# Routing of a mixture-of-experts layer: experts compared in every group beside the group choice, running counts by doubling, slot positions of the chosen experts only, one-hot tables in halves, single-pass products

## What is computed

```python
p_group = softmax(t @ w_rg + b_rg); top_p, top_g = top_k(p_group, 1)
inner_logits = einsum('td,gde->tge', t, w_re) + b_re
sel_logits = einsum('tge,tg->te', inner_logits, one_hot(top_g))
top_l, top_e = top_k(sel_logits, 2); top_w = softmax(top_l)
gate = one_hot(top_g) * top_p  x  sum_k top_w[k] * one_hot(top_e[k])
for e in range(16):
    a, u = split(t @ w_ei[e], 2)
    y += gate[:, e] * ((silu(a) * u) @ w_eo[e])
```

## Time and profile before

| | us |
|---|---|
| median of 3 runs | 1457.71 (1456.18 to 1462.59) |
| profiled execution, its own time | 1458.04 |
| its span in the profile | 1456.3 |

### The profile page before, as it was taken

How to read it: one execution, slowest core, us unless ns; L and a number is a source line. 1 busy time by engine, 2 the same in 40 slices (tenths; PEclk the granted TensorE clock), 3 DMA queues, 4 the chain that set the end, 5 groups by cost and what they waited for, 6 DMA issues and landing times.

```text
span 1456.3 us, 20186 instructions
## 1 busy us (share of the span) xinstructions
PE 1291.3 (89%) x7662; PEld 1074.6 (74%) x7663; DVE 787.1 (54%) x956; ACT 640.7 (44%) x872; POOL 271.7 (19%) x279
## 2 busy tenths in 40 slices
PE   5999998899998999998899997388999999899960
PEld 4788756788798888756688797366787778778850
DVE  3333488321664432378421665577856775985546
ACT  2322456422322322465422322367745564775434
POOL 0432000000200232000000200134522323652210
PEclk9999999999999999999999997589999999999985
DMA  7773300044572444300045563379977987996416
GB/s 173 230 168 87 87 1 2 1 93 138 127 221 88 93 107 90 87 1 2 1 88 144 119 206 122 135 244 309 329 222 224 335 263 258 314 362 221 139 36 244
DMA packets 58464, 222.41 MB, mean 153 GB/s; under 512 B 12087, under 2 KB 12599, under 8 KB 50935
## 3 DMA queue, kind: packets, MB, share of 16 engines
q1 hardware_dynamic: 43088, 177.40, 40.9%
q0 software_dynamic: 12192, 34.51, 8.4%
q10 hardware_dynamic: 3116, 9.54, 1.7%
HBM read 200.19 MB, written 34.32 MB: 161 GB/s over the span
## 4 chain that ended last, share of the span: by engine, by line
PE 71%; DVE 11%; ACT 7%; issue 6%; DMA 3%; POOL 1%; SPq 0%; ACTq 0%; POOLq 0%; DVEq 0%
PE banks L658 20%; PE banks L659 20%; PE banks L660 20%; ACT qkvA L1159 2%; PE banks L868 2%; ACT moe_hi L1199 2%; PE banks L940 2%; DVE pt L1451 2%; DVE moe_lo L1341 1%; PE banks L792 1%; PE banks L826 1%; PE banks L861 1%; DVE neg_max L1419 1%; DMA raw<-in_front_w 1%; POOL gated L567 1%
## 5 line engine op out<-in xcount | busy, mean ns | idle before, releaser
L1341 DVE TENSOR_TENSOR moe_lo<-moe_raw,moe_hi 128x2048 fp32r<-128x2048 f32 x102 | 233.1, 2289 | 78.9 <-ACT moe_hi L1199 75.8
L1354 DVE TENSOR_TENSOR wlo<-raw,whi 128x2048 fp32r<-128x2048 f32 (+1 forms) x52 | 116.1, 2232 | 185.2 <-ACT whi L1049 185.2
L1199 ACT ACTIVATE moe_hi<-moe_raw 128x2048 fp32r<-128x2048 f32 x102 | 194.7, 1914 | 43.6 <-PE banks L660 38.9
L658 PE MATMUL banks<-xT,whi 128*128 128x512 f32 x448 | 175.2, 391 | 0.0
L659 PE MATMUL banks<-xT,whi 128*128 128x512 f32 x448 | 175.0, 391 | 0.0
L660 PE MATMUL banks<-xT,wlo 128*128 128x512 f32 x448 | 175.0, 391 | 0.0
L658 PE MATMUL banks<-moe_lo,xeh 128*128 128x512 f32 x368 | 148.1, 403 | 9.0 <-issue 4.7
L658 PE MATMUL banks<-wlo,xT 128*128 128x256 f32 x512 | 148.8, 291 | 6.9 <-DVE xT L1478 6.7
L659 PE MATMUL banks<-whi,xT 128*128 128x256 f32 x512 | 146.6, 286 | 0.0
L660 PE MATMUL banks<-whi,xT 128*128 128x256 f32 x512 | 146.5, 286 | 0.0
L659 PE MATMUL banks<-moe_hi,xeh 128*128 128x512 f32 x368 | 145.5, 396 | 0.0
(11 more groups left out here) (242 smaller groups left out, 2422.0 us busy)
## 6 DMA issues: line engine op xcount, KB each, us to landing
moe_raw<-in_expert_w SPq DMA_DIRECT2D x192, 512.0 KB
raw<-in_front_w SPq DMA_DIRECT2D x104, 512.0 KB, 6.8
toeplitz_rows<-bias_rows POOLq DMA_DIRECT2D x4, 1152.0 KB, 15.8
kqv<-in_x SPq DMA_DIRECT2D x8, 512.0 KB, 10.9
pt<-in_x SPq DMA_DIRECT2D x2, 2048.0 KB, 9.5
x_rows<-pt ACTq DMA_DIRECT2D x8, 512.0 KB, 2.7
token_sums<-pt ACTq DMA_DIRECT2D x8, 512.0 KB, 3.6
sum_tile<-token_sums SPq DMA_DIRECT2D x8, 512.0 KB, 8.6
```

Of the source, the lines that this page charges most:

```text
L658: mm(dst, left[0], right[1], start=first, stop=False)
L1199: A(moe_hi[m % SPLIT_E], moe_raw[m % RAW_E], ACT.Copy).then_inc(e_hi, 1)
L1341: V.tensor_tensor(moe_lo[m % SPLIT_E], moe_raw[m % RAW_E], moe_hi[m % SPLIT_E].bitcast(F32), ALU.subtract).then_inc(e_lo, 1)
L1354: V.tensor_tensor(view(lo, shape), view(raw[c % 2], shape), view(hi, shape).bitcast(F32), ALU.subtract).then_inc(w_split, 1)
```

## The change

It rewrites the routing and moves work around it.

- The best and the second expert are sought in all four groups at once (128x128 tiles), beside the search for the group; `run` and `done` let two such chains take turns on DVE.
- Running counts come from three additions of 128x128 (`pairs`, `fours`, `upto_t`) in place of eight of 128x16. The rank product waits for the membership, the one for the counts for a second signal; DVE's next step waits for these two products and no longer for the totals.
- Positions are worked out for the 16 chosen pairs of tile and choice only, from rank and base by two multiply-and-sum steps.
- `hot_lo` and `hot_col` are made in halves of 128x1024, in turns; ACT and PE start on a half. `hot_token` and `hot_col` are stored as fp32r, so that the token products are one pass of TensorE each.
- Gates and the experts' counts are worked out behind the one-hots, counts behind the slot table.
- DVE splits two weight chunks ahead of the routing and two behind the slot table; ACT puts the last `store_x1` and `keep_x1` between its first three splits.
- POOL issues the second pair of gathers when the first pair has landed.

```diff
-            nc.alloc_sbuf_tensor_at(name, [P, 2 * NT * P], F32, offset=place_at)[:, :].rearrange("p (n i) -> p n i", n=2 * NT)
-            for name, place_at in (("hot_lo", hot_at), ("hot_gate", hot_at + W_BYTES),
-                                   ("hot_col", late_at), ("hot_token", late_at + W_BYTES))]
+            nc.alloc_sbuf_tensor_at(name, [P, 2 * NT * P], dt, offset=place_at)[:, :].rearrange("p (n i) -> p n i", n=2 * NT)
+            for name, dt, place_at in (("hot_lo", F32, hot_at), ("hot_gate", F32, hot_at + W_BYTES),
+                                       ("hot_col", F32R, late_at), ("hot_token", F32R, late_at + W_BYTES))]
...
             pool.wait_ge(x1_out, 16 * NT + 1)
             for b in range(2):
+                if b == 1:
+                    pool.wait_ge(rows_in[0], 32)
                 for c in range(2):
                     nc.gpsimd.indirect_dma_start(
                         out=x_rows[b][:, c * D:(c + 1) * D], out_offset=None, in_=x1_d[:, :],
...
-            mm(bank[2][:, 0:M16], before, rt[:, 0:M16], start=True, stop=False)
-            mm(bank[2][:, 0:M16], ones, rt[:, M16:2 * M16], start=False, stop=True)
-            mm(bank[3][:, 0:NE], ones, rt[:, 2 * M16:2 * M16 + NE], start=True, stop=True).then_inc(ranked, 1)
+            mm(bank[2][:, 0:M16], before, member_t, start=True, stop=False)
+            pe.wait_ge(member, 2)
+            mm(bank[2][:, 0:M16], ones, upto_t, start=False, stop=True).then_inc(ranked, 1)
+            mm(bank[3][:, 0:NE], ones, upto_t[:, M16 - NE:M16], start=True, stop=True).then_inc(ranked, 1)
             for a in range(2):
                 for n in range(2 * NT):
-                    pe.wait_ge(hot_ready, 2)
+                    pe.wait_ge(hot_ready, 2 + 2 * (n // NT))
                     pe.wait_ge(weighted, 2 * NT * a + n + 1)
-                    last = mm(bank[4 + a][:, 0:FULL_COL], hot_w[a][:, n], hot_col[:, n], start=(n == 0), stop=(n == 2 * NT - 1))
+                    last = mm(bank[4 + a][:, 0:FULL_COL], hot_w[a][:, n], hot_col[:, n] if a == 0 else hot_col[:, n].bitcast(F32),
+                              start=(n == 0), stop=(n == 2 * NT - 1))
                 last.then_inc(tabled, 1)
...
-                if s == SEQS - 1:
-                    store_x1(s, 3)
-                    keep_x1(s, 3)
...
-            for c in range(EARLY_E):
-                e_split(0, c)
+            e_split(0, 0)
+            store_x1(SEQS - 1, 3)
+            e_split(0, 1)
+            keep_x1(SEQS - 1, 3)
+            e_split(0, 2)
...
             for k, weight in enumerate((token, gate)):
-                act.wait_ge(hot_ready, 1)
                 for n in range(2 * NT):
+                    act.wait_ge(hot_ready, 1 + 2 * (n // NT))
...
-                    for c in range(EARLY_E):
-                        e_split(0, c)
+                    for o in (0, R_PAIRS - 4 * NE, R_FOURS - 4 * NE):
+                        V.memset(rt[:, o:o + 4 * NE], 0.0).then_inc(zeroed, 1)
+                    V.memset(small[:, 58:60], 0.0)
+                    e_split(0, 0)
+                    e_split(0, 1)
...
-            chain(V.memset(rt[:, M16:M16 + NE], 0.0))
-            for j in range(1, NT + 1):
-                o = M16 + j * NE
-                ins = V.tensor_tensor(rt[:, o:o + NE], rt[:, o - NE:o], rt[:, (j - 1) * NE:j * NE], ALU.add)
-                if j < NT:
-                    chain(ins)
-            ins.then_inc(member, 1)
...
+            n_e = run(V.tensor_reduce(t4(best), lg_e, X, ALU.max))
+            n_g = run(V.tensor_reduce(g_max, lg_g, X, ALU.max))
+            done(n_e)
+            n_e = run(V.tensor_tensor(t44(e_tmp), lg_e, over_e(best), ALU.is_equal))
+            done(n_g)
+            n_g = run(V.tensor_tensor(t4(g_tmp), lg_g, over_4(g_max), ALU.is_equal))
+            V.tensor_tensor(t4(g4), lg_g, over_4(g_max), ALU.subtract).then_inc(r_exp_in, 1)
+            done(n_e)
+            n_e = run(V.tensor_tensor(t44(e_tmp), t44(e_tmp), tie_e, ALU.mult))
+            done(n_g)
+            n_g = run(V.tensor_tensor(t4(g_tmp), t4(g_tmp), tie_g, ALU.mult))
...
+            done(n_e)
+            chain(V.tensor_tensor(t44(hot2), t44(e_tmp), over_e(e_tie), ALU.is_equal))
+            chain(V.tensor_tensor(e_tmp, hot1, hot2, ALU.add))
+            V.tensor_tensor(t44(member_t), t44(e_tmp), over_e(g_hot), ALU.mult).then_inc(member, 1)
...
+            chain(V.tensor_tensor(pairs, member_t, rt[:, R_MEMBER - NE:R_MEMBER - NE + M16], ALU.add))
+            chain(V.tensor_tensor(fours, pairs, rt[:, R_PAIRS - 2 * NE:R_PAIRS - 2 * NE + M16], ALU.add))
+            V.tensor_tensor(upto_t, fours, rt[:, R_FOURS - 4 * NE:R_FOURS - 4 * NE + M16], ALU.add).then_inc(member, 1)
+
+            V.tensor_tensor(t44(one1), t44(hot1), over_e(g_hot), ALU.mult)
+            chain(V.tensor_tensor(t44(one2), t44(hot2), over_e(g_hot), ALU.mult))
+            prod, base = r(2 * M16), r(2 * NT)
...
+            chain(V.tensor_tensor(by_expert(prod), by_expert(ones12), expert_base.unsqueeze(1).broadcast_to([P, 2 * NT, NE]), ALU.mult))
+            chain(V.tensor_reduce(base, by_expert(prod), X, ALU.add))
...
-            chain(V.tensor_scalar(where, wv, float(SLOTS), float((NE - 1) * SLOTS), ALU.is_ge, ALU.mult))
-            for k in (2, 3):
-                chain(V.tensor_scalar(prod, wv, float(SLOTS * k), float((NE - 1) * SLOTS), ALU.is_ge, ALU.mult))
-                tt(where, where, prod, ALU.add)
-            tt(where, where, wv, ALU.add)
-            eb = expert_base.unsqueeze(1).broadcast_to([P, NT, NE])
-            tt(where.rearrange("p (t e) -> p t e", e=NE), where.rearrange("p (t e) -> p t e", e=NE), eb, ALU.add)
-            for k, one in enumerate((one1, one2)):
-                tt(prod, one, where, ALU.mult)
-                chain(V.tensor_reduce(tmp[:, k * NT:(k + 1) * NT], prod.rearrange("p (t e) -> p t e", e=NE), X, ALU.add))
...
+            chain(V.tensor_tensor(prod.rearrange("p (k m) -> p k m", k=2), ones12.rearrange("p (k m) -> p k m", k=2),
+                                  bank[2][:, 0:M16].unsqueeze(1).broadcast_to([P, 2, M16]), ALU.mult))
+            chain(V.tensor_reduce(rank, by_expert(prod), X, ALU.add))
+            chain(V.tensor_copy(rank_i, rank))
+            n_lo = run(V.tensor_scalar(lo_i, rank_i, P - 1, None, ALU.bitwise_and))
+            n_col = run(V.tensor_scalar(col_i, rank_i, 7, None, ALU.logical_shift_right))
+            n_over = run(V.tensor_scalar(pass_i, rank_i, 8, None, ALU.logical_shift_right))
+            done(n_lo)
+            n_lo = run(V.tensor_copy(lo_f, lo_i))
+            done(n_col)
+            n_col = run(V.tensor_copy(col_f, col_i))
+            done(n_over)
+            chain(V.tensor_copy(pass_f, pass_i))
+            n_col = run(V.scalar_tensor_tensor(col_f, pass_f, float((NE - 1) * SLOTS // P), col_f, ALU.mult, ALU.add))
...
-            for hot, number in ((hot_lo, lo_f), (hot_col, col_f)):
-                V.tensor_tensor(hot, iota.unsqueeze(1).broadcast_to([P, 2 * NT, P]),
-                                number.unsqueeze(2).broadcast_to([P, 2 * NT, P]), ALU.is_equal).then_inc(hot_ready, 1)
...
+                part = slice(k * NT, (k + 1) * NT)
+                V.tensor_tensor(hot[:, part], iota.unsqueeze(1).broadcast_to([P, NT, P]),
+                                number[:, part].unsqueeze(2).broadcast_to([P, NT, P]), ALU.is_equal).then_inc(hot_ready, 1)
+
+            done(n_lo)
+            one_hot(hot_lo, lo_f, 0)
+            done(n_col)
+            chain(V.scalar_tensor_tensor(col_f, base, 1.0 / P, col_f, ALU.mult, ALU.add))
+            one_hot(hot_col, col_f, 0)
+            one_hot(hot_lo, lo_f, 1)
+            one_hot(hot_col, col_f, 1)
...
-            V.memset(slot_v[:, FULL_COL:, 0], 0)
-            V.memset(slot_v[:, FULL_COL:, 1], NOWHERE)
-            chain(V.memset(slot_v[:, FULL_COL:, 2], 0))
-            dve.wait_ge(tabled, 1)
-            chain(V.tensor_scalar(slot_v[:, 0:FULL_COL, 1], bank[4][:, 0:FULL_COL], float(NOWHERE), None, ALU.add))
-            V.tensor_scalar(slot_v[:, 0:FULL_COL, 0], slot_v[:, 0:FULL_COL, 1], MAXTOK - 1, None, ALU.bitwise_and).then_inc(table_ready, 1)
...
-            for c in range(EARLY_E, RAW_E):
+            for c in range(2, RAW_E):
```

More of the change, by code:

```diff
@@ L166 @@
 SLOT_W = 3
-NOWHERE = 4 * MAXTOK
+NOWHERE = MAXTOK
 XCH = 4
@@ L1623, in _, with t44 @@
[L1623 to L1629 removed]
+            def t44(a):
+                return a.rearrange("p (t g e) -> p t g e", g=4, e=4)
```

137 lines of the change are left out of this document (83 added, 54 removed).

## The result

The changed kernel takes 1444.65 us (median of 6 runs, 1444.10 to 1446.89) where the kernel before takes 1456.92 beside it (6 runs, 1449.28 to 1462.59): a ratio of 0.9919, 95% interval 0.9904 to 0.9934. That is a gain of 12 us where 16.4 were forecast: inside the stated range of 1438 to 1448, 3 us above the number (1441.5), and 0.65 us outside the 1439 to 1444 that the forecast's own case had.

A forecast was written before the change was run, and what follows sets the result against it. The routing's chain, 899.69 to 951.48 us with no second engine beside it, was taken as the bound. Five terms of 4.6, 2.8, 2.0, 4.5 and 2.5 sum to 16.4 us less, about 1441.5; range 1438 to 1448.

The forecast's parts named there:

- the forecast's own case: Routing chain: all five terms come as reckoned, about 1441.5 us, range 1439 to 1444; chance 0.59.
- (a): Gathers late: second gather blocked by both splits, sharing DMA engines with chunk 6 and table's store; 1444 to 1447.5; chance 0.15.
- (b): Routing: no overlap between DVE's steps, and one-pass products bring nothing; gain 12 to 14, 1444 to 1446 us; chance 0.07.
- Term 1: Start of the routing's search: the last logit decides instead of the splits, search begins at 903.9; -4.6 us.
- Term 2: Search and membership: the group's 32-column steps run in the shadow of 128-column ones, 7.24 to 4.4 us; -2.8 us.
- term 3: Membership to one-hots: fewer, partly unwaited DVE steps, third product off the path, 6.15 to 4.2 us; -2.0 us.
- Term 4: One-hots to slot table: tables in halves and one-pass products, 11.34 to 6.8 us, upper bound 8.4; -4.5 us.
- Term 5: Slot table to gathered rows: first gather free, second blocked 1.7, landing 5.0; 12.05 to 9.5 us; -2.5 us.
- (c): Slot table to rows, more than forecast: second gather not blocked, lands after 4.4 us; 2.3 more gained, 1439; chance 0.08.
- (d): Experts give the gain back because their first chunks come later than the rows; 1450.5 to 1457 us; chance 0.08.
- (e): Slower: DVE stands at the experts' loop entry for the second pair of gathers; 1467 if landing takes 35 us; chance 0.03.

The follow-up runs named there:

- splits behind: Changed kernel with DVE's third and fourth weight-chunk splits moved behind the work on the gathered rows (xel): 1442.48 us, 0.9901 of the kernel before.
- Four gathers at once: Changed kernel without POOL's wait between the two pairs of gathers, all four issued at once: 1442.75 us, one run.
- no turns: Changed kernel with every DVE instruction that takes turns made to wait for its own end, order unchanged: 1444.88 us.
- two-pass products: Changed kernel with hot_token and hot_col stored as fp32 again, so each token product has two passes: 1445.24 us.
- loads held: Changed kernel with SP loading weight chunks 6 and later only once the first gathers landed: 1439.03 us (0.9873); repeated, 1441.17 us (0.9897).

## Why the prediction was right, and where it missed

The total does not tell the cases apart: 1444.65 lies in the bands of rivals (a) and (b) and just outside the forecast's own. The stages do.

**Term 1** (forecast -4.6) came out at -4.6 by the stage. The last logits decide, as said. That the search began at 903.65 where 903.9 was forecast is in part luck: the changed kernel's other profiled execution began it at 901.42. ACT's order carries nearly all of the term; with it, the third split could have stayed ahead of the last logits for 0.2 us, and chunk 6's load with it, away from the gathers.

**Term 2** (-2.8) measured -3.0, **term 3** (-2.0) measured -1.9. The bookkeeping of a step at duration + 0.04 with a wait, duration - 0.08 without, held through some 40 steps. Without the turns these two terms would be 2.7 us less. The Trainium skill (VectorE: DVE Perf Modes, "The DRAIN you can't avoid") has the next instruction start only when the pipe is empty, and excepts one that is not held. By the first half nothing would overlap, and the trace disagrees: the changed kernel's rows start 0.21 us after a step of 0.29.

**Term 4** (-4.5) measured -4.4. One pass gives 1.4 us and halves 1.6. The pass costs 0.23 to 0.25 where I took 0.21. For the first eight products that is covered, since PE waits for `hot_col` behind them; for the last eight it is 0.3 us (they end 6.9 after the first one-hot's start, not 6.55), which covers the term's miss of 0.2.

**Term 5** (-2.5) is the step that failed, by its size and its sign: +0.5. It had three parts. The first gather free (1.08 instead of 2.28) and the second blocked (2.25 instead of 0.97) was right; the loss was 1.3 us and not 1.7, since the gather started later under the split. The Trainium skill's rule (SBUF — State Buffer, "Who interferes with whom"), a VectorE instruction with two SBUF inputs against a GpSimd instruction that reads SBUF, holds for it. The same section reports that a probe's `tensor_tensor` did not stall a DMA; for these gathers the measurement decides: with a split beside it the gather takes 2.24 us, without 0.96 to 0.97. That also settles what one pair of rows had left open: it is no matter of a first call.

The second part, the landing, was "5.0", being 7.9 less 2.9 for the two later gathers, now held back. The size was right for a gather with no load beside it (splits behind: from 919.39 to 924.45 us, 5.1), the reason wrong. Four gathers at once changed nothing; what stood beside the gathers in the kernel before and was not reckoned with was chunk 7's load, and the change did not take it away but added chunk 6's. That this one load made the 2.9 us of the kernel before is an inference: no run holds it back there. The third part was missing: I had placed SP's loads of chunks 6 and 7 in time ("both land before the experts start"), asked only whether they were late for their user, and not what they did to the gathers beside them. They cost 3.5 and 3.1 us, which is the miss of 3.0. Held back, the gather lands 6.2 us after its start, half a microsecond better than the 6.7 forecast.

**Rivals.** (a), at a chance of 0.15, had the better account of this stage: the gathers share the DMA engines with a weight load, and the landing takes 8.6 us; without the blocking it took 8.4 (921.99 to 931.66, less 1.3). Its other half, being blocked by both splits, did not come: the gather ended 1.3 us late, before the second split was through. (b) is refuted, by no turns for the steps and by two-pass products for the pass. (c), (d) and (e) didn't come: the experts' +0.5 is inside the spread, PE's one wait there for `moe_lo` (2.7 us) stood in the kernel before too (2.4), and DVE's loop did not stand for the second pair. Rival (d)'s mechanism is real all the same: in the trace of "splits behind" it took back what the early rows had gained.

**Behind**: rows to first product 6.16 as forecast, PE 422.3 busy in the experts' 448.5 us as before. The sum has a slip of 0.2 us that changes nothing: 1457.71 less 16.4 is 1441.3, not 1441.5.

## What to carry to other kernels

A transfer that only has to be early enough for its user can still be too early: when an edit frees a buffer sooner, ask which transfer that starts, and whether one on the critical path is under way then; a wait on SP gave back 3 us here, and its user's stage stayed inside its spread. In a chain of small steps on one engine, find a second independent chain and let the two take turns, and size the gain by which steps keep a wait. Ask what releases a stage before counting the work of its own engine in front of it: most of term 1 lay on another engine's order. And when a row's duration is split up among causes, list every transfer that was under way beside it; here the one left out was the one that counted.

## What the runs showed of the hardware

- Two more gathers on the software queue did not delay the ones ahead of them: with them the first rows came 11.02 us after the first gather, without 11.06 and 10.70. Two weight loads of 1 MB on the hardware queue beside them cost 3.1 to 3.5 us.
- A split of 128x2048 by DVE blocks more than a gather. In the changed kernel a one-column operation of POOL, 0.19 us in the kernel before with no split beside it, took 2.04 under a split that began at 938.68 and ended at 941.0, and the gather behind it stood under the next one:

```profile
938.68 4.49 DVE L1350 TENSOR_TENSOR moe_lo<-moe_raw,moe_hi 128x2048 fp32r<-128x2048 f32 x2 [1.11 <-ACT moe_hi L1203]
...
938.99 2.04 POOL L617 TENSOR_TENSOR wait_bearer<-wait_bearer 128x1 f32<-128x1 f32 x1 [1.64 <-DMA slot_ids<-slots]
941.19 2.90 POOL L598 DMA_INDIRECT x_rows<-x_rows,slot_ids  x1 [0.16 <-issue]
```

- In these traces the longer wait cost TensorE its clock. The windows' view (PEclk is the third number from the end) of the wait for rows and of the turning, for the changed kernel and then with loads held:

```profile
924.00:931.60 7.60, 0.09 (x1) 0.00 (x0) 1.59 (x1) 0.35 (x1) 0.23 (x1) 0.81 0.87 266
931.60:936.30 4.70, 3.91 (x16) 3.06 (x16) 1.65 (x3) 1.83 (x4) 3.08 (x5) 0.50 0.95 320
```

```profile
922.00:926.20 4.20, 0.15 (x2) 0.00 (x0) 1.68 (x1) 0.35 (x1) 0.32 (x1) 1.00 0.53 205
926.20:930.40 4.20, 3.43 (x16) 2.61 (x16) 1.63 (x3) 1.81 (x4) 3.64 (x6) 0.57 0.68 180
```

  After 7.6 us of standing still the turning begins at 0.50 (1.2 GHz) and the first eight records take 1.97 us; after 4.1 us the grant is still 1.00 (2.4 GHz) as they begin, and they take 1.49 (1.10 with the splits behind, after 2.9). That is where row to first product fell from 6.16 to 5.70: rows that come early are also turned faster.
